# Half of a mixer's last stages set beside an expert gather, and an index lookup in two passes instead of three

## The reference, cut to what matters

```python
# block 1, end of the mixer: h is per token from here on
x = x + gt1 * ((g_mla * (o_mla @ w_o_mla) + g_rwkv * (o_rwkv @ w_o_rwkv)) @ w_out)
h = rms_norm(x, norm_ffn) * (1 + sc2) + sh2
# experts
q = h @ w_query                       # 8 heads x 2 halves x 128
v1, i1 = top_k(q[..., 0, :] @ keys1.T, 16);  v2, i2 = top_k(q[..., 1, :] @ keys2.T, 16)
top_v, pos = top_k(v1[..., :, None] + v2[..., None, :], 16)   # 16 of 256 pairs
expert = i1[pos // 16] * 128 + i2[pos % 16]
x = x + gt2 * sum(softmax(top_v) * gelu(h . down[expert]) * up[expert])
```

## Time and profile before

| what | value |
|---|---|
| median of 3 runs | 4061.76 us (4057.13 to 4063.77) |
| the profiled execution | 4057.91 us, its span 4056.1 us |
| mean granted TensorE clock (1 is 2.4 GHz) | 0.825 |
| DMA moved | 1247.03 MB, of it 1073.81 MB by the gather's queue |
| busy share of the span | PE 76%, DVE 59%, POOL 29%, ACT 22% |

### The profile page before, as it was taken

The page is one execution under the profiler, slowest core; times in us unless marked ns, Lnnn a source line. Parts: engine busy times, 40 slices in busy tenths (PEclk is TensorE's granted clock), DMA queues, the critical chain, the costliest instruction groups (busy, mean ns, idle before and its releaser), DMA issues. The chain is left out here.

```text
span 4056.1 us, 49859 instructions
## 1 busy us (share of the span) xinstructions
PE 3071.0 (76%) x18158; PEld 1490.0 (37%) x18158; DVE 2393.2 (59%) x6092; ACT 911.5 (22%) x2477; POOL 1164.3 (29%) x1029
## 2 busy tenths in 40 slices
PE   5976596884676665889798875989798876666766
PEld 4853493541221111543365531633365531111111
DVE  6557634337746777456645479456745478755554
ACT  2113231101211111126512111126512111111111
POOL 0000000003443444323333333322333334444342
PEclk8998698896787777987899986988999987766666
DMA  5510002118999999988899997987999999999998
GB/s 210 186 66 1 6 4 68 56 63 340 401 409 377 414 418 414 379 345 318 335 416 370 345 393 307 360 331 253 339 416 380 345 390 398 416 420 418 420 420 351
DMA packets 201682, 1247.03 MB, mean 307 GB/s; under 512 B 25108, under 2 KB 28820, under 8 KB 66980
## 3 DMA queue, kind: packets, MB, share of 16 engines
q0 software_dynamic: 147456, 1073.81, 66.1%
q1 hardware_dynamic: 53992, 170.17, 11.4%
HBM read 1239.39 MB, written 4.46 MB: 307 GB/s over the span
## 5 line engine op out<-in xcount | busy, mean ns | idle before, releaser
L263 PE MATMUL held_acc<-held_pair,held_diag 64*64 64x512 f32 x8192 | 1408.1, 784 | 591.9 <-ACT held_diag L289 559.9
L243 POOL DMA_INDIRECT held_pair<-in_experts,held_expert x1024 | 1160.5, 1133 | 2373.4 <-PE held_acc L263 1822.1
L309 DVE CUSTOM_DVE_ANT_0 held_pair<-held_pair,held_hrow 128x1024 f32<-128x1024 f32 x1024 | 1248.4, 1223 | 790.8 <-DMA held_pair<-in_experts,held_expert 782.6
L263 PEld LDWEIGHTS held_acc<-held_pair,held_diag 64*64 64x64 f32 x8192 | 269.4, 158 | 1458.2 <-ACT held_diag L289 1254.8
L289 ACT ACTIVATE held_diag<-held_bands,held_weight 128x64 f32<-128x64 f32 x1024 | 347.8, 340 | 1424.4 <-DVE held_weight L304 1423.7
L282 ACT ACTIVATE held_bent<-held_dot 128x2 f32<-128x2 f32 x512 | 104.0, 203 | 755.4 <-DVE held_dot L309 738.2
L1768 PE MATMUL c_ps<-held_hT,c_w 128*128 128x256 f32 (+1 forms) x480 | 146.9, 460 | 0.0
L645 PE MATMUL pgh_ps<-held_hT,pgh_w 128*128 128x256 f32 x608 | 142.9, 389 | 5.1 <-DMA pgh_w<-in_w_in 5.1
L1250 POOL TENSOR_TENSOR rsolve_decays<-rsolve_ident,rwkv_dend 128x2048 f32<-128x2048 f32 x1 | 3.6, 3610 | 488.8 <-DMA rsolve_ident<-in_id 488.8
L645 PE MATMUL p2h_ps<-held_hT,p2h_w 128*128 128x256 f32 x576 | 134.0, 386 | 0.0
L645 PEld LDWEIGHTS pgh_ps<-held_hT,pgh_w 128*128 128x128 f32 x608 | 113.6, 192 | 48.7 <-issue 27.6
(11 more groups left out here) (475 smaller groups left out, 3660.6 us busy)
## 6 DMA issues: line engine op xcount, KB each, us to landing
pgh_w<-in_w_in SPq DMA_DIRECT2D x38, 512.0 KB, 8.2
p2h_w<-in_w_in SPq DMA_DIRECT2D x36, 512.0 KB, 7.8
p_raw<-in_w_in SPq DMA_DIRECT2D x34, 512.0 KB, 3.6
p_w_ada<-in_w_ada SPq DMA_DIRECT2D x16, 1024.0 KB, 7.1
held_pair<-in_experts,held_expert POOLq DMA_INDIRECT x1024, 10.5
held_first_tile<-in_w_in SPq DMA_DIRECT2D x20, 512.0 KB, 7.9
c_w<-in_w_peer_q SPq DMA_DIRECT2D x20, 512.0 KB, 7.8
ada_w<-in_w_ada SPq DMA_DIRECT2D x4, 2048.0 KB, 18.4
```

Of the source, the lines that this page charges most:

```text
L243: pool.indirect_dma_start(self.pair[m % BUFS][:], None, self.layers[t // TT][0], bass.IndirectOffsetOnAxis(ap=self.expert[:, t % TT, s:s + ...
L263: last = pe.matmul(self.sum_of(i)[to * BAND:(to + 1) * BAND], diag[band, :], up[band, turn * WIDE:(turn + 1) * WIDE], start=s == 0, stop=s ...
L309: ins = dve.tensor_tensor_reduce(down, down, self.hrow[:, t % TT, :], 1.0, 0.0, ALU.mult, ALU.add, self.dot[:, t % 2, s:s + 1])
```

## The change

The stages of block 1 from the merge on are cut by tokens. "mga", "poa", "n2a" and the queries "c0" now handle tokens 0 to 255 alone, and then the gather starts. The same work for tokens 256 to 511 ("mgb", "pob", "n2b", "c2") becomes stages beside beats 0 to 266, after the memory stages; `choose_stage` is gone and tiles 2 and 3 are chosen in "c2". `FIRST_LENGTHS` is the new division of the beats. The second half's projection uses `project_beside_stage` (plain float32 matmuls). ACT copies the late halves of the two branches into `hT` and the sigmoids of the late gates into `room` during "mga". Weights `w_o_mla`, `w_o_rwkv` (2 MB each), `w_out` (4 MB) and `w_query` (8 MB) are read twice. To make room, `z` stays allocated and holds `room`, four of the eight `pair` buffers and the first weight tile. The lookup takes two passes: with ids i[n] in 0..127 and wanted position p, it forms i[n] + 512n - 512p and takes the smallest absolute value over n.

```diff
-PIECES = 21
+PIECES = 19
+APART = 4 * NK
...
             link(dve.tensor_copy(idf[:], idx[:]))
+            link(dve.tensor_scalar(partf[:], partf[:], float(APART), None, ALU.mult))
+            link(dve.tensor_tensor(idf[:], idf[:], bcast(self.steps[:], 2 * PH, 1), ALU.add))
         elif i < PIECES - 1:
-            u, step = divmod(i - CENTRED_AT - 1, 3)
+            u, step = divmod(i - CENTRED_AT - 1, 2)
...
+            wanted = bcast(partf[:, u].rearrange("p (h n) -> p h n", h=PH), K16, 3)
             if step == 0:
-                link(dve.tensor_tensor(hit[:], bcast(partf[:, u], K16, 2), bcast(self.iota[:], NJ, 1), ALU.is_equal))
-            elif step == 1:
-                link(dve.tensor_tensor(hit4, hit4, bcast(id4[:, :, u, :], K16, 2), ALU.mult))
+                link(dve.tensor_tensor(hit4, bcast(id4[:, :, u, :], K16, 2), wanted, ALU.subtract))
             else:
-                link(dve.reduce_sum(found[:, u, :], hit[:], AX))
+                link(dve.tensor_reduce(found[:, u, :], hit[:], AX, ALU.min, apply_absolute_value=True))
...
+FIRST_LENGTHS = {"choose1": 56, "mn": 7, "mp": 14, "mh": 14, "mt": 4, "mg": 15, "po": 13, "n2": 6, "query": 82, "choose": 55}
...
-    beats = shared_out(gather, 0, half_done, {"choose1": 62, "mn": 8, "mp": 50, "mh": 12, "mt": 4, "choose": 144})
-    query_stage(nc, "c0", k, ins, gather, ins["w_query"], hT, qT, S, ins["keys1"], keys_of_first, [at(0), at(1)], [at(t) for t in range(TT)],
+    beats = shared_out(gather, 0, half_done, FIRST_LENGTHS)
...
+    query_stage(nc, "c0", k, ins, gather, ins["w_query"], hT[:, :, early], qT, HALF, ins["keys1"], keys_of_first, [(0, 0), (1, P)], [(0, 0), (1, P)],
...
-        choose_stage(nc, "c23", k, ins, gather, qT, ins["keys1"], keys_of_first, [at(2), at(3)], beats["choose"],
-                     [(memory[:, 0:4, :], mkv[:, 0:4, :]), (memory[:, 4:8, :], mv[:].rearrange("p h j n -> p h (j n)"))])
...
+        merge_stage(nc, "mgb", gates, 0, [(ins["w_o_mla"], hT[:, 0:4, late]), (ins["w_o_rwkv"], hT[:, 4:8, late])], hT[:, :, early],
+                    tokens=HALF, beats=beats["mg"], fetch=store, squashes=False)
+    project_beside_stage(nc, "pob", ins["w_out"], hT[:, :, early], DC, DC, xT[:, :, late], HALF, beats["po"], first_tile,
+                         add=(mod[:, 2 * DC:3 * DC], xT[:, :, late]))
+    norm_stage(nc, "n2b", k, xT[:, :, late], DC, D, gain, hT[:, :, late], shift=mod[:, 3 * DC:4 * DC], tokens=HALF, beats=beats["n2"],
+               fetch=lambda sp: first_tile.fetch(sp, ins["w_query"]))
+    query_stage(nc, "c2", k, ins, gather, ins["w_query"], hT[:, :, late], room[:, 0:2 * PH, :], HALF, ins["keys1"], keys_of_first,
+                [(2, 0), (3, P)], [(2, 0), (3, P)], beats["query"], beats["choose"], first_tile)
...
-                merge_stage(nc, "mg1", z, Z_GATE, [(ins["w_o_mla"], oT), (ins["w_o_rwkv"], yT)], hT)
-            project_stage(nc, "po1", k, ins["w_out"], hT, DC, DC, xT, add=(mod[:, 2 * DC:3 * DC], xT))
+                kept = [(hT[:, 0:4, late], oT[:, :, late], ACT.Copy), (hT[:, 4:8, late], yT[:, :, late], ACT.Copy)]
+                kept += [(room[:, c, :], z[:, Z_GATE + c, late], ACT.Sigmoid) for c in range(2 * DC)]
+                merge_stage(nc, "mga", z[:, :, first_half], Z_GATE, [(ins["w_o_mla"], oT[:, :, first_half]), (ins["w_o_rwkv"], yT[:, :, first_half])],
+                            hT[:, :, first_half], tokens=HALF, kept=kept)
+            project_stage(nc, "poa", k, ins["w_out"], hT[:, :, first_half], DC, DC, xT[:, :, first_half], tokens=HALF, add=(mod[:, 2 * DC:3 * DC], xT[:, :, first_half]))
```

More of the change, by code:

```diff
@@ L199, with __init__ @@
 class FirstTile:
-    def __init__(self, r):
-        self.tile, self.landed, self.count = r.sb("first_tile", [P, DC, P]), r.sem("first_landed"), 0
+    def __init__(self, r, tile):
+        self.tile, self.landed, self.count = tile, r.sem("first_landed"), 0
     def fetch(self, sp, w_dram):
@@ L210, with __init__ @@
 class Gather:
-    def __init__(self, r, k, xT, layers):
+    def __init__(self, r, k, xT, layers, pairs):
         self.k, self.xT, self.layers = k, xT, layers
         self.hrow, self.sums = r.sb("hrow", [P, TT, D]), r.sb("sums", [P, D])
-        self.pair = [r.sb(f"pair{u}", [P, 2 * D]) for u in range(BUFS)]
+        self.pair = pairs + [r.sb(f"pair{u}", [P, 2 * D])[:] for u in range(len(pairs), BUFS)]
         self.diag = [r.sb(f"diag{u}", [P, BAND]) for u in range(DIAGS)]
@@ L1491, in _, with merge_stage @@
                     dve.tensor_tensor(yt[:, t], yt[:, t], ps[t][:], ALU.mult).then_inc(rows, 1)
-def merge_stage(nc, name, z, gate0, branches, out, kc=4, bias=None, tokens=S, beats=None, fetch=None):
+def merge_stage(nc, name, z, gate0, branches, out, kc=4, bias=None, tokens=S, beats=None, fetch=None, squashes=True, kept=()):
     nb = len(branches)
@@ L1522, in _ @@
             def _(act):
-                for m in range(DC):
+                for m in range(DC if squashes else 0):
                     for i in range(nb):
@@ L1527, in _ @@
                         act.activation(gate, gate, ACT.Sigmoid, **extra).then_inc(squashed, 1)
+                for dst, src, func in kept:
+                    act.activation(dst, src, func)
                 for n in range(nb * DC):
@@ L2135, in experts_and_second_mixer @@
     keys_of_second = lambda c: c
-    at = lambda t: (t, t % TT * P)
-    qT = room[:].rearrange("p (c u) n -> p c (u n)", u=S // HALF)
-    gather = Gather(r, k, xT, layers)
-    beats = shared_out(gather, 0, half_done, {"choose1": 62, "mn": 8, "mp": 50, "mh": 12, "mt": 4, "choose": 144})
-    query_stage(nc, "c0", k, ins, gather, ins["w_query"], hT, qT, S, ins["keys1"], keys_of_first, [at(0), at(1)], [at(t) for t in range(TT)],
-                Beats(), beats["choose1"], first_tile, load=(memory_halves(hT)[0], ins["memT"].rearrange("(c p) t -> p c t", p=P)))
@@ new lines, in experts_and_second_mixer, with store @@
+    early, late = slice(0, HALF), slice(HALF, S)
+    gates, qT, mkv = room[:, 0:2 * DC, :], room[:, 2 * DC:2 * DC + 2 * PH, :], room[:, 2 * DC:3 * DC, :]
+    mT = hT[:, :, early]
+    query_stage(nc, "c0", k, ins, gather, ins["w_query"], hT[:, :, early], qT, HALF, ins["keys1"], keys_of_first, [(0, 0), (1, P)], [(0, 0), (1, P)],
+                Beats(), beats["choose1"], first_tile, load=(mT, ins["memT"].rearrange("(c p) t -> p c t", p=P)))
+    with ExitStack() as stack:
+        m = Room(nc, stack, "mem")
+        mv, stored = m.sb("mv", [P, 4, 2, P]), m.sem("memory_stored")
+        memory_stages(nc, k, ins, cols, mT, mkv, mv, beats, first_tile)
+        def store(sp):
+            sp.dma_start(memory[:, 0:4, :], mkv[:, 0:4, :]).then_inc(stored, 16)
+            sp.dma_start(memory[:, 4:8, :], mv[:].rearrange("p h j n -> p h (j n)")).then_inc(stored, 16)
+            first_tile.fetch(sp, ins["w_out"])
+            sp.wait_ge(stored, 32)
+        merge_stage(nc, "mgb", gates, 0, [(ins["w_o_mla"], hT[:, 0:4, late]), (ins["w_o_rwkv"], hT[:, 4:8, late])], hT[:, :, early],
+                    tokens=HALF, beats=beats["mg"], fetch=store, squashes=False)
@@ L2182, in build @@
         sc = r.sb("silu", [P, DC])
+        z = r.sb("z", [P, Z_N, S])
+        rstd = z[:, Z_ROPE, :]
+        room = z[:, 0:Z_GD, :].rearrange("p a (u n) -> p (a u) n", n=HALF)
+        first_half, late = slice(0, HALF), slice(HALF, S)
         loads = [(k.ident[:], ins["ident"]), (k.causal[:], ins["causal"]), (k.pair_ones[:], ins["pair_ones"]), (k.bands[:], ins["bands"])]
@@ L2224, in build @@
                 rwkv_finish_stage(nc, k, ins, y_of(rT), vT[:], bonus, sgate, yT, None)
-                merge_stage(nc, "mg1", z, Z_GATE, [(ins["w_o_mla"], oT), (ins["w_o_rwkv"], yT)], hT)
-            project_stage(nc, "po1", k, ins["w_out"], hT, DC, DC, xT, add=(mod[:, 2 * DC:3 * DC], xT))
+                kept = [(hT[:, 0:4, late], oT[:, :, late], ACT.Copy), (hT[:, 4:8, late], yT[:, :, late], ACT.Copy)]
[3 more added lines that the diff above has]
+            project_stage(nc, "poa", k, ins["w_out"], hT[:, :, first_half], DC, DC, xT[:, :, first_half], tokens=HALF, add=(mod[:, 2 * DC:3 * DC], xT[:, :, first_half]))
         gain_stage(nc, "g2", gain, cols("norm_ffn"), mod[:, 4 * DC:5 * DC])
-        first_tile = FirstTile(r)
-        norm_stage(nc, "n2", k, xT, DC, D, gain, hT, shift=mod[:, 3 * DC:4 * DC], fetch=lambda sp: first_tile.fetch(sp, ins["w_query"]))
-        experts_and_second_mixer(nc, r, k, ins, cols, xT, hT, mod, first_tile)
+        first_tile = FirstTile(r, z[:, Z_ROPE - 1:Z_N, :].rearrange("p a (c n) -> p (a c) n", n=P))
+        pairs = [z[:, Z_GD + 4 * u:Z_GD + 4 * u + 4, :].rearrange("p a n -> p (a n)") for u in range(4)]
+        norm_stage(nc, "n2a", k, xT[:, :, first_half], DC, D, gain, hT[:, :, first_half], tokens=HALF, shift=mod[:, 3 * DC:4 * DC], fetch=lambda sp: first_tile.fetch(sp, ins["w_query"]))
+        experts_and_second_mixer(nc, r, k, ins, cols, xT, hT, mod, gain, room, pairs, first_tile)
         with ExitStack() as stack:
```

24 lines of the change are left out of this document (9 added, 15 removed).

## The result

| | before | changed |
|---|---|---|
| median | 4062.77 us of 4 runs (4057.13 to 4076.18) | 3991.72 us of 4 runs (3985.09 to 3994.14) |
| ratio | | 0.9824, 95% interval 0.9807 to 0.9841 |
| profiled execution, its span | 4057.91, 4056.1 us | 3991.26, 3989.4 us |
| DMA moved | 1247.03 MB | 1263.90 MB |

A forecast was written before the change was run, and what follows sets the result against it. A front of some 928 us without a gather, then a stream bound by transfers in its first and last parts and by work beside it in the mixer halves. -116 + 50 - 4 = -70 us gives 3988, by median 3992; range 3962 to 4024.

The forecast's parts named there:

- go round once in two chunks: 3.4 us: Front, projection "poa": a loop of weight load, high part and low part, 6.8 us per two chunks, sets the chunk time.
- First part: Stream's beats 0 to 266: grows by 50 us to 757 from added weight reads and moved stages; bounds 28 and 90.
- with 16 units and 15 beats 54: Late merge "mgb": 54 us, from the mixer's merge of 79 us with 24 units and 20 beats.
- 3 for the squeezed memory projection: Memory stages in the stream's first part: 3 us extra because the memory projection gets 14 beats instead of 48.
- 0 to 5 us, in the 54: Late merge "mgb": two stores and the next weight load queue behind the last merge weights, costing 0 to 5 us.
- 82 x 2.54 + 8.4 MB / 0.415 + 2: Late query stage "c2": 82 beats plus the time for w_query's bytes read again, 231 us.
- Later parts: After the first part: the shorter lookup saves 3.9 us beside the choice of tile 5, nothing elsewhere; bounds 0 and 10.
- B: Rival: new stages dip from late weights and drained buffers; first part grows 80 to 100 us, time 4022 to 4042; chance 0.12.
- C: Rival: weight loads don't overlap, so a half-size projection chunk takes 7.1 us, 13 us worse in all; time 4023; chance 0.05.
- The rule quoted in the prediction: Projection matmuls: a weight load overlaps running matmuls only when its row group differs; half-size chunks would then cost more.
- D: Rival: 116 beats beside the new stages fall to 3.53 us each, 409 instead of 352; 4049; decides from 422; slower, 0.02.
- E: Rival: the gather gains more, the first part grows by only 25 to 35 us; time 3965 to 3977; chance 0.13.

The follow-up runs named there:

- experiment 5: Changed kernel with one of three partial products left out in "poa", 16 matmuls a chunk instead of 24: 3981.73 us in one run.
- the repeat: The changed kernel measured once more, unaltered, on another chip: 3985.53 us, ratio 0.9826 to the kernel before.
- experiment 6: Changed kernel with the first weights of both branches of "mgb" loaded early, during the memory's head norm: 3981.51 us, ratio 0.9827 to the kernel before.
- experiment 7: Changed kernel with first weights of "mgb" and the second mixer's two merges loaded early, and w_out's first tile before the stores: 3977.97 us, ratio 0.9818.
- experiment 9: As experiment 7, with the two stores of the memory's keys and values moved from "mgb" to "n2b": 3976.71 us, ratio 0.981 to the kernel before.
- Experiment 3: Changed kernel loading only an eighth of w_query's weights in "c2" after the first three loads: 3991.74 us, ratio 0.9853 to the kernel before.
- experiment 8: Changed kernel with twelve further 512 KB loads in "c2" into buffers nobody reads: 3997.57 us, ratio 0.9851 to the kernel before.
- experiment 2: Changed kernel with the three-pass lookup put back: 4008.65 us, ratio 0.9892 to the kernel before.

## Why the prediction was right, and where it was not

**Merge: right.** 27.8 us saved, forecast 28; units every 1.72 us. PE never waits for ACT's copies and sigmoids; DVE does once, 10.9 us at the stage's start, without holding PE.

**Projection: a term mis-sized.** 22.7 saved, forecast 18. The step was "go round once in two chunks: 3.4 us" for the loads. It gave a load with issue and semaphores 6.8 - 1.06 - 1.22 = 4.5 us; in the changed kernel the one that can be read took 3.4, a loop of 2.9 a chunk, and experiment 5 shows loops of 3.0 and 3.2. PE, at 24 x 120 ns = 2.88, decides by a hair. The forecast's upper bound, 22, was slightly passed.

**Norm, queries, lookup: right.** 8.9 (10), 55.7 (56) and 4.1 (3.9). Weight loads and DVE's copies stayed hidden, and the new reduction costs what the sum cost. Front in all 119.2 instead of 116.

**First part: a term mis-sized.** It grew by 64 us in the first trace and by 58 in the repeat (765.0 - 707.4), forecast 50. What the runs show of the difference: first the merge's head, 6 to 7 us (experiment 6). The step "with 16 units and 15 beats 54" scaled the mixer's whole merge, 79 us, and with it the wait for its first weights, 7.6 us there; but that wait comes once a stage, whatever the units, and was 11.0 us here. A PE that waits for weights also stops the stream whose buffers it frees.

Second, the norm's stage took 23.1 us, not 18; in the repeat 19.8. Third, the stages before the merge took 8 us more than forecast. The write of tile 1's indices (948.72) divides them: the choice takes 141.5 us, where its 56 beats at 2.61 make 147, and the memory stages 127.8, where 39 beats with the forecast's 10 + 3 make 115. So the term "3 for the squeezed memory projection", with the 10 for its weights, was too small by some 13 us. The stream's rate dips there, in the memory's norm, projection and head norm, to 348, 385 and 362 GB/s (columns as in the earlier trace rows):

```profile
956.00:977.00 21.00, 15.73 (x72) 7.30 (x72) 14.11 (x27) 8.01 (x22) 6.73 (x7) 0.69 0.88 348
977.00:1026.00 49.00, 44.31 (x240) 28.34 (x240) 20.87 (x44) 5.67 (x22) 16.69 (x14) 0.97 0.97 385
1026.00:1062.00 36.00, 25.64 (x116) 6.38 (x120) 19.09 (x43) 8.92 (x25) 14.58 (x13) 0.66 0.93 362
```

In the projection PE is busy 44 of 49 us. What each dip costs no experiment isolates. The term "0 to 5 us, in the 54" for the stores held: they cost 3 to 5 us by the traces of experiments 6, 7 and 9, and "pob" was no longer than forecast (47.3 against 49).

**The reason for "c2" was wrong, its number nearly right** (224.5 us against 231, the beats after it 147.4 against 144). The step "82 x 2.54 + 8.4 MB / 0.415 + 2" takes the bytes as the only bound. Experiment 3 took two thirds of those bytes away and gained nothing; experiment 8 added three quarters of them and lost 11 to 12 us. Two bounds of about equal length lay there, and a sum over either comes out near that length: that the number fits is luck.

**Later parts: 3.95 us of the 9.6 are settled.** The choice of tile 5, from the indices of tile 4 to its own, first before, then after:

```profile
2459.76 0.29 DVE L1672 SCALAR_TENSOR_TENSOR held_expert<-c_found 128x128 uint32<-128x128 f32 x1
...
2532.11 0.29 DVE L1672 SCALAR_TENSOR_TENSOR held_expert<-c_found 128x128 uint32<-128x128 f32 x1
```

```profile
2395.46 0.29 DVE L1677 SCALAR_TENSOR_TENSOR held_expert<-c_found 128x128 uint32<-128x128 f32 x1
...
2463.87 0.29 DVE L1677 SCALAR_TENSOR_TENSOR held_expert<-c_found 128x128 uint32<-128x128 f32 x1
```

72.35 and 68.41 us. Every version with two passes shows 68.4, the one with three 72.4. The other 5.6 us are a difference: from the second mixer's first weight load to the indices of tile 4 it took 824.2 us before and 817.0 after, and behind the first mixer half 1.6 us more. The lookup isn't needed for it, as experiment 2 with three passes shows 818.0. Nor is one trace of each enough: the first mixer half took 877.9 to 890.9 us in eight traces of kernels that are alike there. Open.

**The sum.** 119.2 saved and 1.7 of earlier start, less 63.8, plus 9.6: 66.7 us, the difference of the two spans. The forecast's -116 + 50 - 4 = -70 came this near partly by luck: the front saved 3 us more, the merge started 2 us earlier and the later parts gave 6 more than thought, and the first part took 14 more. In the repeat those 14 are 8.

**The rivals.** B (dips) was half there: the dips exist, but the first part outgrew the forecast by only 8 to 14 us, not by 30 to 50. C is refuted: 24 matmuls in 2.88 us, 120 ns each, with a weight load per matmul that shows as 192 ns in the median. Tile `poa_ps`, columns as in the earlier trace rows:

```profile
L547 PEld LDWEIGHTS poa_ps<-poa_hlo,poa_whi x64: 188/192/338, 675.9 to 699.9; 128*128 128x128 f32 x64
```

The rule quoted in the prediction does not hold here. The Trainium skill (TensorE: Matmul & The Clock Gate, section "Step-by-step: what each phase is for") has a second condition under which a weight load overlaps, a load into the background weight buffer. The 120 ns are in line with that one; the buffer itself no trace shows. D is refuted: the 116 beats beside merge, projection, norm and queries took 59.7 + 47.3 + 23.1 + 224.5 = 355 us, or 3.06 a beat, near the forecast's 352 and far from the 422 where it decides. E did not happen in the first part, which grew by 58 to 64 and not by 25 to 35. (From 25 to 35 the time would follow as 3967 to 3977; the 3965 of the text is 2 us off.)

## What to carry to other kernels

Work moved beside a transfer-bound stream costs little more than its bytes only until the loop of the engines is as long as the transfers. Price both bounds, and test the price from both sides (take bytes away, add bytes), because a sum that fits doesn't show which one holds. When a stage is scaled to fewer units, take its once-only parts out first, such as the wait for its first weights. Where transfers bound the stream, a stage that starts with a weight load stops the stream as well, if the engine that waits is the one that frees the stream's buffers: load its first weights one stage earlier, and keep slow stores away from the end of its block (6 to 7 and 3 to 5 us here). Where the work beside the stream was the bound, the same step showed no gain (experiment 7). And when an instruction's width is halved, look for the next loop (loads, splits) and measure it from step to step in the middle of the stage, on a run in which the engine is not the bound.
